# Sharing one pass of the input projection between two prompt tiles and the sample in a decoder layer with an expert stream

## The chip, the cores and the metric
One core of a Trainium2 chip. The metric is the device time of one execution of the kernel, in microseconds, as the median of several runs.

## What is computed
One layer of a decoder for a prompt of 512 tokens and a sample of 8 sequences with 4 new tokens each, width 1024, all in float32:

```python
h = rms_norm(x, norm1) * (1 + sc1) + sh1
zq, zkc, zvc, zks, zvs, zkw, zvw, zg, zglu = split(h @ w_in)     # 1024 -> 2328 columns
# attention: compressed blocks, selected blocks, window; the conv branch: glu, depthwise 31 taps
mix = concat([rms_norm(o_attn), o_conv * scale]) @ w_out
x = x + gt1 * mix
h2 = rms_norm(x, norm2) * (1 + sc2) + sh2
x = x + gt2 * peer(h2)       # per token 8 heads x 16 of 16384 experts: gather u and v rows, dot, gelu, weigh, sum
```

The keys and values, the last 30 columns of the convolution's input, and the layer's rows are outputs. `compress` turns 32 key rows into one through a hidden layer with the weights `cmp_w1` (4 MiB for keys and values).

## The kernel before, in words
The 544 token rows are cut into five tiles: four of the prompt (128 rows each) and the sample (32 rows). Each tile goes through the stages x (norm, modulate, turn), glu, z (q, k, w products, norms, turns), conv, cmp (compression), att (8 heads), mix (output projection and first residual), query0 and query1 (the experts' query projection and scores) and topk0, topk1 (the choice of 128 experts a token). The sample has sc (four parts: compression of the cached pages) and satt in place of cmp and att.

Two streams share the engines. The **expert rows**: GpSimd gathers u and v of one chosen expert for each of 128 tokens (1 MiB, line 1964) into a ring of ten buffers; DVE makes the dot product (line 1920), ScalarE gelu and a diagonal (lines 1400 to 1416), TensorE the weighted sum (line 1053, two rows of the plan at a time), which frees the buffer. One gather is one **row of the plan**: 128 for each prompt tile, 32 for the sample (which packs four heads' groups of 32 tokens), 544 in all. FIRST[i] is the first row of tile i: 0, 128, 256, 384, 512. The **side work**: the stages of the next tile, written as generators that yield at the end of a slot. Each engine runs the same sequence of slots in order, between its instructions for the rows; PE takes its slots four rows ahead.

`make_plan` (L412) lists the stages in windows: a list of lists holds lanes that go side by side. `SLOTS_OF` (L399) gives for each stage its slots and its length in rows, `size_of` that of att by tile (16, 26, 30, 40). `slots_before` (L446) searches a pace so that all lengths together, times the pace, end at row 500; within an item all slots are evenly spaced. An item holding lanes has the length of its first lane. mix of tile i may not begin before row FIRST[i-1] + 8. Tile 0's side work runs before the first row.

Weights come in **units** of 1 MiB (256 columns of a matrix), through three slots; SyncE loads unit j when unit j-3 has been used, in the order of `weight_units`. For every tile these are four glu units, five z units, four compression units, four of `w_out`, eight of `peer_q`, and two half units of keys. `aside` (L2087) hangs everything else that SyncE does on a unit, ahead of its load: `load_x` at a tile's first glu unit, `store_z` and `store_y(i-2)`, `load_y(i-1)` and the modulation rows at its first `w_out` unit. SyncE waits in order, so whatever stands in `aside` holds up the units behind it.

PSUM banks 4 to 7 are the side work's, given in turn to each product (`Products`, L88). `stage_room` is one SBUF area that all stages share by time. At a tile's last row ScalarE and DVE read the sums out of banks 0 to 3 (L1383 to L1910) before PE starts the next tile's rows (the wait on `s_ye`).

## Time and profile before

| what | value |
|---|---|
| median of 3 runs | 2131.38 us |
| lowest and highest | 2120.32, 2132.27 us |
| the profiled execution's own time | 2122.48 us |
| its span on the core | 2120.8 us |
| granted TensorE clock, mean | 0.814 |
| first and last dot product | 263.7 and 2104.4 us from the span's start |
| DMA traffic | 782 MB |

All rows below are of that one profiled execution. A window's line gives for each engine the busy microseconds and the number of instructions that lie in it; TensorE shows two records for every float32 matmul. "DMA share" is the mean busy share of the sixteen DMA engines.

### The profile page before, as it was taken

How to read it: one execution, taken by the hardware profiler on the slowest of the kernel's cores; microseconds unless marked ns; L12 is line 12 of the kernel's file. 1: busy time of each engine (PE TensorE's matmuls, PEld its weight loads, DVE VectorE, ACT ScalarE, POOL GpSimd, SP SyncE). 2: the span in 40 equal slices, each digit the busy share in tenths (PEclk: the TensorE clock that was granted, in tenths of full speed). 3: DMA queues.
4: the chain of work that ended last, by engine and by line, in shares of the span. 5: the costliest groups of instructions: out<-in, count | busy, mean ns of one | idle time of the engine just before them, and what ended most of it. 6: DMA issues, size and time to landing. Idle time of an engine off the chain costs nothing.

```text
span 2120.8 us, 29350 instructions
## 1 busy us (share of the span) xinstructions
PE 1529.5 (72%) x9952; PEld 883.9 (42%) x9952; DVE 1239.4 (58%) x3327; ACT 781.9 (37%) x2225; POOL 698.6 (33%) x611
## 2 busy tenths in 40 slices
PE   6686468777768876868795675989687776769533
PEld 4556335334534444644252353545254332436100
DVE  0151685784686884686797359653555454443754
ACT  2231154662244754255483332252412232332322
POOL 0840122332323432323434232344323333323442
PEclk7877779778978877979797797979888878878765
DMA  7764999988999978999999989999989989999996
GB/s 280 272 251 160 370 375 420 399 315 331 421 415 397 413 326 355 377 386 422 424 386 420 425 365 371 399 419 393 424 319 377 406 327 342 367 413 384 414 413 275
DMA packets 149993, 782.09 MB, mean 369 GB/s; under 512 B 17392, under 2 KB 53136, under 8 KB 60932
## 3 DMA queue, kind: packets, MB, share of 16 engines
q0 software_dynamic: 78336, 570.46, 65.5%
q1 hardware_dynamic: 71509, 209.77, 25.9%
q8 instruction: 80, 1.31, 0.2%
q14 instruction: 68, 0.56, 0.1%
HBM read 773.75 MB, written 10.99 MB: 370 GB/s over the span
## 4 chain that ended last, share of the span: by engine, by line
PE 22%; DMA 13%; DVE 8%; issue 6%; SPq 3%; ACT 3%; POOL 1%; POOLq 0%; ACTq 0%; DVEq 0%
PE bank L1053 9%; DMA expert_rows<-in_expert_uv,expert_index 8%; PE bank L930 5%; DVE expert_rows L1920 3%; PE bank L857 2%; PE bank L841 1%; SPq L2007 1%; PE bank L675 1%; SPq L2002 1%; DMA weight_units<-in_win_values 1%; DMA weight_units<-in_win_keys 1%; DMA weight_units<-in_w_out_units 1%; DMA gate_or_shift_and_scale<-mod_dram 1%; PE bank L647 1%; PE bank L1056 1%
## 5 line engine op out<-in xcount | busy, mean ns | idle before, releaser
L1964 POOL DMA_INDIRECT expert_rows<-in_expert_uv,expert_index x544 | 626.5, 1152 | 1333.9 <-PE bank L1053 1090.0
L1920 DVE CUSTOM_DVE_ANT_0 expert_rows<-expert_rows,h_rows 128x1024 f32<-128x1024 f32 x544 | 658.6, 1223 | 383.2 <-DMA expert_rows<-in_expert_uv,expert_index 376.0
L1053 PE MATMUL bank<-expert_rows,weight_diagonals 64*64 64x512 f32 x4096 | 600.6, 713 | 120.4 <-ACT weight_diagonals L1416 95.2
L1400 ACT ACTIVATE group_gelu<-group_dots 128x2 f32<-128x2 f32 x272 | 55.2, 203 | 788.0 <-DVE group_dots L1920 748.0
L1053 PEld LDWEIGHTS bank<-expert_rows,weight_diagonals 64*64 64x64 f32 x4096 | 152.4, 153 | 396.4 <-issue 223.8
L857 PEld LDWEIGHTS bank<-stage_room,weight_units 128*128 128x128 f32 x1280 | 153.6, 200 | 40.4 <-issue 31.2
L1416 ACT ACTIVATE weight_diagonals<-consts_sb,group_weights 128x64 f32<-128x64 f32 (+1 forms) x544 | 158.1, 338 | 20.0 <-PE bank L1053 2.5
L857 PE MATMUL bank<-stage_room,weight_units 128*128 128x128 f32 (+1 forms) x1280 | 160.7, 286 | 5.7 <-DMA weight_units<-in_peer_q_units 3.1
L1406 ACT ACTIVATE group_weights<-group_gelu,expert_gate 128x1 f32<-128x1 f32 x544 | 130.5, 287 | 9.4
L930 PE MATMUL bank<-weight_units,prompt_bias 128*128 128x256 f32 x512 | 129.5, 404 | 0.0
L1532 DVE SCALAR_TENSOR_TENSOR conv_out<-stage_room,small_weights,conv_out 128x128 f32<-128x128 f32 (+1 forms) x480 | 125.4, 319 | 0.0
L930 PEld LDWEIGHTS bank<-weight_units,prompt_bias 128*128 128x128 f32 x512 | 97.8, 199 | 38.8 <-issue 26.5
L841 PE MATMUL bank<-weight_units,stage_room 128*128 128x256 f32 (+1 forms) x320 | 82.3, 419 | 29.8 <-DVE stage_room L1676 15.4
L1400 ACT ACT_TABLE_LOAD x80 | 102.6, 1283 | 1.4
L675 PE MATMUL bank<-weight_units,stage_room 128*128 128x256 f32 (+1 forms) x400 | 92.5, 386 | 3.1 <-DMA weight_units<-in_w_in_units 3.1
L647 PEld LDWEIGHTS bank<-stage_room,weight_units 128*128 128x128 f32 x640 | 75.3, 197 | 23.4 <-issue 15.9
L841 PEld LDWEIGHTS bank<-weight_units,stage_room 128*128 128x128 f32 (+1 forms) x320 | 60.6, 194 | 56.0 <-DVE stage_room L1676 17.9
L675 PEld LDWEIGHTS bank<-weight_units,stage_room 128*128 128x128 f32 (+1 forms) x400 | 68.6, 176 | 33.7 <-issue 15.2
L647 PE MATMUL bank<-stage_room,weight_units 128*128 128x128 f32 (+1 forms) x640 | 78.5, 283 | 4.3 <-ACT stage_room L1118 3.8
L1056 PE MATMUL bank<-expert_rows,weight_diagonals 128*32 128x512 f32 x128 | 29.1, 1059 | 54.7 <-ACT weight_diagonals L1416 43.3
L1225 ACT ACTIVATE stage_room<-stage_room,stats 128x128 f32<-128x128 f32 (+7 forms) x96 | 44.8, 468 | 50.5 <-DVE stats L1632 50.4
L780 PE MATMUL bank<-prompt_keys_values,queries_turned 64*128 64x128 f32 (+3 forms) x128 | 56.4, 551 | 5.0 <-ACT stage_room L1238 3.4
(253 smaller groups left out, 1606.6 us busy)
## 6 DMA issues: line engine op xcount, KB each, us to landing
weight_units<-in_w_in_units SPq DMA_DIRECT2D x45, 1024.0 KB
weight_units<-in_peer_q_units SPq DMA_DIRECT2D x40, 1024.0 KB
weight_units<-in_w_ada_units SPq DMA_DIRECT2D x24, 1024.0 KB
weight_units<-in_w_out_units SPq DMA_DIRECT2D x20, 1024.0 KB
weight_units<-in_w_units SPq DMA_DIRECT2D x16, 1024.0 KB
expert_rows<-in_expert_uv,expert_index POOLq DMA_INDIRECT x544
weight_units<-in_cmp_pages SPq DMA_DIRECT2D x128, 64.0 KB
gate_or_shift_and_scale<-mod_dram SPq DMA_DIRECT2D x12, 512.0 KB
```

Source lines behind the costliest of these rows:

```text
L647: last = mm(out[:, a * P:a * P + r], w[:, k, a * P:(a + 1) * P], hT(i, k), start=(k == 0), stop=(k == KD - 1))
L675: last = mm(out[0:r, c * 256:(c + 1) * 256], hT(i, k), w[:, k], start=(k == 0), stop=(k == KD - 1))
L841: last = mm(out[0:r, 0:256], e.catT[:, k, 0:r], w[:, k], start=(k == 0), stop=(k == KD - 1))
L857: last = mm(out[:, c:c + r], w[:, k, a * P:(a + 1) * P], e.h2T[:, k, 0:r], start=(k == 0), stop=(k == KD - 1))
L930: last = mm(dst, e.w1_s[:, one, s, hh * P:(hh + 1) * P], w[:, :, :, s], start=False, stop=(one == 1 and s == 7))
L1053: last = mm(e.bank[2 * a + c][o * HD:(o + 1) * HD, :], e.diag[ps, m % (NG * GR)], e.ring[ps, m % RING, cs], start=first, stop=final)
L1400: do(e.act_v[:, p], e.dots[:, p], ACT.Gelu_apprx_tanh).then_inc(e.s_gelu, 1)
L1406: do(e.wv[:, p, j:j + 1], e.act_v[:, p, j:j + 1], ACT.Copy, scale=e.gsm[:, i % 2, o + j:o + j + 1]).then_inc(e.s_w, 1)
L1416: do(e.diag[:, p * GR + j, 0:unit.shape[1]], unit, ACT.Copy, scale=e.wv[:, p, j:j + 1]).then_inc(e.s_d, 1)
L1532: ins = vec.scalar_tensor_tensor(out, src, w[:, ct, k:k + 1], out, ALU.mult, ALU.add)
L1920: vec.tensor_tensor_reduce(out=row, in0=row, in1=e.h2[:, i % 2], scale=1.0, scalar=0.0, op0=ALU.mult, op1=ALU.add, accum_out=e.dots[:, q % ...
L1964: pool.indirect_dma_start(e.ring[:, n % RING], None, e.io["expert_uv"], bass.IndirectOffsetOnAxis(ap=e.eidx[:, i % 2, j:j + 1], axis=0)).t ...
```

## The change
Tiles 2, 3 and the sample ("the team", 288 tokens) are normed one after the other through the one x buffer and go through glu and z together: each glu unit is multiplied with 288 columns at once, each z unit is used for three tiles before it is given back. The compression's four units serve tiles 2 and 3. Tile 3's queries and convolution input wait in DRAM until its attention; the sample's u and queries stay in small tiles; x of the three tiles is loaded again for the residual. All stores of the three tiles' keys and values come ahead of tile 2's first `w_out` unit. The plan's window of tile 3 begins with topk1 of tile 2 and attention 3, beside the convolution; that of the sample begins with sc. Cut to its core:

```diff
+LATE = 2
+TEAM = tuple(range(LATE, TILES))
+TOKENS = sum(rows(t) for t in TEAM)
+
+
+def columns(i, k):
+
+    if i < LATE:
+        return slice(k * P, (k + 1) * P)
+    a = k * TOKENS + (i - LATE) * P
+    return slice(a, a + rows(i))
+
+
+Z_ORDER = ([(n, i) for i in range(LATE) for n in ("q", "k", "w", "cmp")]
+           + [(n, i) for n in ("q", "k", "w") for i in TEAM] + [("cmp", PT - 1), ("sc", 0), ("sc", 1)])
+KEYS_NORMED = [z for z in Z_ORDER if z[0] in ("k", "w")]
+
+
+def keys_normed(name, i):
+    return KEYS_NORMED.index((name, i)) + 1
+
+
+def x_loads(i):
+    return 16 * (i + 1 if i < LATE else TILES + i - LATE + 1)
...
+    team = mods[:].rearrange("p o n -> p (o n)")
+    e.eb_team = team[:, 0:2 * TOKENS].rearrange("p (a n) -> p a n", a=2)
+    e.u3 = team[:, 2 * TOKENS:2 * TOKENS + 4 * P].rearrange("p (c n) -> p c n", c=4)
+    e.q3 = team[:, 2 * TOKENS + 4 * P:2 * TOKENS + 8 * P]
...
+    e.hT = room[:, 0:KD * TOKENS]
+    e.ht = [room[:, 1024:2048]] * LATE + [room[:, 4416:5440]] * len(TEAM)
+    at = [2048] * LATE + [KD * TOKENS + 512 * (i - LATE) for i in TEAM]
+    e.zc = [room[:, a:a + 384] for a in at]
+    e.zw = [room[:, a + 384:a + 512] for a in at]
+    e.sq = [room[:, 2560:3072]] * LATE + [e.convo[:].rearrange("p c n -> p (c n)")] * len(TEAM)
+    e.qr = [room[:, 3072:3584]] * LATE + [e.attn[:]] * len(TEAM)
...
+TEAM_SLOTS = {"glu": (18, 14), "z": (38, 22), "cmp": (15, 8)}
...
-    for i in range(2, PT):
-        windows.append(chain(i, []))
-    windows.append([[[("sc", 0), ("x", PT), ("glu", PT)], [("topk1", PT - 1)]], ("sc", 1), ("z", PT),
+    windows.append(chain(LATE, []))
+    windows[-1][0][0][1:1] = [("x", i) for i in TEAM[1:]]
+    i = PT - 1
+    windows.append([[[("topk1", i - 1), ("att", i)], [("conv", i)]],
+                    ("mix", i), ("query0", i), [[("query1", i)], [("topk0", i)]]])
+    windows.append([[[("sc", 0)], [("topk1", PT - 1)]], ("sc", 1),
                     [[("sc", 2), ("sc", 3), ("satt", PT)], [("conv", PT)]],
                     ("mix", PT), ("query0", PT), ("query1", PT), ("topk0", PT)])
...
+    def glu_team(i):
+        for t in TEAM:
+            prod.freed(pe, ("hT", t, 0))
+            prod.freed(pe, ("hT", t, 1))
+        for ct in range(4):
+            w = units.take(("in", i, 5 + ct)).rearrange("p (k n) -> p k n", k=KD)
+            for a in range(2):
+                out = prod.open(pe, ("glu", i, ct, a))
+                for k in range(KD):
+                    last = mm(out[:, 0:TOKENS], w[:, k, a * P:(a + 1) * P], e.hT[:, k * TOKENS:(k + 1) * TOKENS],
+                              start=(k == 0), stop=(k == KD - 1))
+                    if k == 3:
+                        yield
+                last.then_inc(prod.ready, 1)
+                if a == 0:
+                    yield
+            units.used_by(("glu", i, ct, 1))
+            yield
...
+        new_u(PT - 1)
+        new_u(PT)
+        ws = [unit(0), unit(1)]
+        yield from product("q", ws, LATE, False, False)
+        yield
+        yield from product("q", ws, LATE + 1, False, False)
+        turn_q(LATE)
+        yield
+        yield from product("q", ws, PT, False, True)
+        turn_q(LATE + 1)
+        yield
+        ws = [unit(2), unit(3)]
+        yield from product("k", ws, LATE, False, False)
+        turn_q(PT)
+        yield
+        yield from product("k", ws, LATE + 1, False, False)
+        yield
+        turn_k(LATE)
+        yield from product("k", ws, PT, False, True)
+        yield
+        turn_k(LATE + 1)
+        ws = [unit(4)]
+        yield from product("w", ws, LATE, True, False)
+        yield
+        turn_k(PT)
+        yield from product("w", ws, LATE + 1, True, False)
+        yield
+        turn_w(LATE)
+        yield from product("w", ws, PT, True, True)
+        yield
+        turn_w(LATE + 1)
+        yield
+        yield
+        yield
+        turn_w(PT)
...
+                for t, out in zip(tiles, outs):
+                    lo = blocks_of(t)[0]
+                    for s in range(8):
+                        j = 32 * (s % 4)
+                        last = mm(out[j:j + 32, 0:256],
+                                  e.rT[:, kv, s, lo + one:lo + one + 16].rearrange("p c g -> p (c g)"),
+                                  w[:, s], start=(one == 0 and s < 4), stop=(one == 1 and s >= 4))
+                    if one:
+                        last.then_inc(prod.ready, 1)
+                    elif t == tiles[-1]:
+                        units.used(last)
+                    if not one or t != tiles[-1]:
+                        yield
+            units.used_by(("part", tiles[-1], kv))
+            yield
...
+        if i > LATE:
+            prod.wait(act, ("hT", i - 1, 1))
+        link(do(e.ht[i][0:r], e.x[0:r], ACT.Square, accum_out=e.st[0:r, 0:1]))
...
+        act.wait_ge(e.s_h2, i)
+        for ct in range(4):
+            for _ in range(4):
+                yield
+            out = prod.wait(act, ("glu", i, ct, 1))
+            if ct >= 2:
+                prod.freed(act, ("glu", i, ct - 2, 0))
+            do(e.eb_team[:, ct % 2], out[:, 0:TOKENS], ACT.Sigmoid).then_inc(prod.free(("glu", i, ct, 1)), 1)
...
+        vec.tensor_copy(e.cu[:, :, 0:CK - 1], e.tail[:])
+        for ct in range(4):
+            for _ in range(4):
+                yield
+            prod.freed(dve, ("glu", i, ct, 1))
+            out = prod.wait(dve, ("glu", i, ct, 0))
+            for t in TEAM:
+                dst = e.cu[:, ct, CK - 1:] if t == LATE else e.u3[:, ct] if t < PT else e.us[:, ct]
+                c = slice((t - LATE) * P, (t - LATE) * P + rows(t))
+                ins = vec.tensor_tensor(dst, out[:, c], e.eb_team[:, ct % 2, c], ALU.mult)
+            ins.then_inc(prod.free(("glu", i, ct, 0)), 1)
...
+        elif i < PT:
+            dve.wait_ge(e.s_ul, 16)
+            link(vec.tensor_copy(e.cu[:, :, 0:CK - 1], e.tail[:]))
+        else:
+            dve.wait_ge(e.s_hist, 16)
+            link(vec.tensor_copy(e.cs[:, :, :, CK - 1:], e.us[:].rearrange("p c (b t) -> p c b t", b=NB)))
...
-            if h == 0 and i == PT - 1:
-                dve.wait_ge(e.s_uo, 16)
-            if h == 1 and i == PT - 1:
-                dve.wait_ge(e.s_zo, 16 * e.z_stores[i])
+            if h == 0 and i == LATE:
+                dve.wait_ge(e.s_uo, 16 * (1 + NB))
+            if h == 1 and i == LATE:
+                dve.wait_ge(e.s_zo, 16 * e.z_stores[PT])
...
-    def load_x(i):
-        if i:
+    def load_x(i, again=False):
+        if again and i == LATE:
+            sp.wait_ge(e.s_h, TILES)
+        elif again or 0 < i <= LATE:
             sp.wait_ge(e.s_h2, i)
             sp.wait_ge(e.s_xo, 16 * i)
+        elif i:
+            sp.wait_ge(e.s_h, i)
...
-        if kind == "in" and key[2] == 3 and i >= PT - 1:
-            store_new_u(i)
+        if key == ("in", LATE, 3):
+            store_new_u(PT - 1)
+            store_new_u(PT)
+        if key == ("in", LATE, 6):
+            load_x(LATE + 1)
+        if key == ("in", LATE, 7):
+            load_x(PT)
+        if key == ("pages", 0, 2):
+            sp.wait_ge(e.s_rt, 2 * PT - 1)
+            sp.dma_start(e.cs, io["conv_history"]).then_inc(e.s_hist, 16)
+            prod.wait(sp, ("o", PT - 1, H - 1))
+            sp.dma_start(e.bias_s, io["bias_sample"][:, 0:PAST + WIN]).then_inc(e.s_sb, 16)
...
-            if 0 < i < PT:
+            if i == 1:
                 store_z(i)
+            if i == LATE:
+                for t in TEAM:
+                    store_z(t)
+                sp.dma_start(e.gate_dram, e.gates[PT][0:NS]).then_inc(e.s_gs, 16)
+                prod.freed(sp, ("q", PT - 1))
+                sp.dma_start(e.q_dram, e.q3).then_inc(e.s_spill, 16)
+                sp.dma_start(e.u_dram, e.u3).then_inc(e.s_spill, 16)
+                sp.wait_ge(e.s_gs, 16)
+                for b in range(NB):
+                    src = bass.AP(e.gate_dram.tensor, b * DT * 3 * H, [[3, H], [3 * H, DT], [1, 3]])
+                    sp.dma_start(e.gates_s[b % 4 * 32:(b % 4 + 1) * 32, b // 4, :], src).then_inc(e.s_gs, 16)
+                sp.wait_ge(e.s_spill, 32)
+            if i == PT - 1:
+                prod.wait(sp, (score_parts(LATE)[-1][0], LATE, H - 1))
+                sp.dma_start(e.qT[:], e.q_dram).then_inc(e.s_ql, 16)
+                sp.wait_ge(e.s_tail, 2)
+                sp.wait_ge(e.s_rt, 2 * LATE + 1)
+                sp.dma_start(e.cu[:, :, CK - 1:], e.u_dram).then_inc(e.s_ul, 16)
+            if i >= LATE:
+                load_x(i, True)
```

Left out: the splitting of the z generators of ACT and DVE into functions for one tile and group (the instructions of one tile are the same), the new semaphores, `modT` and `small` areas used for the sample's queries and gates, and the reordering of the `pe` columns.

## Rows read from the trace of the kernel before
**Rows 1.** The page: DMA share in 40 slices, and the two large queues.
```profile
DMA  7764999988999978999999989999989989999996
...
q0 software_dynamic: 78336, 570.46, 65.5%
q1 hardware_dynamic: 71509, 209.77, 25.9%
```

**Rows 2.** Windows: us, busy us (count) by engine, PEclk, DMA share, GB/s.
```profile
264.00:2104.00 1840.00, 1351.04 (x8653) 749.76 (x8653) 1148.79 (x3014) 715.87 (x2047) 616.93 (x534) 0.82 0.95 387
...
510.00:545.00 35.00, 33.21 (x250) 22.77 (x252) 15.47 (x40) 10.62 (x36) 11.51 (x10) 0.88 0.75 300
...
647.00:677.00 30.00, 27.27 (x201) 17.94 (x203) 14.87 (x32) 19.47 (x48) 10.02 (x8) 1.00 1.01 413
...
726.00:760.00 34.00, 25.48 (x117) 14.87 (x117) 24.12 (x68) 19.04 (x50) 5.30 (x7) 0.60 0.62 250
...
929.00:977.00 48.00, 40.69 (x280) 25.86 (x284) 43.33 (x140) 25.07 (x54) 14.20 (x14) 0.87 0.93 378
...
1006.00:1134.00 128.00, 104.81 (x701) 51.64 (x697) 110.34 (x326) 75.05 (x208) 53.72 (x47) 0.88 0.99 406
...
1134.00:1170.00 36.00, 20.53 (x136) 5.73 (x132) 24.45 (x39) 12.17 (x44) 14.93 (x13) 0.68 1.01 427
...
1170.00:1231.00 61.00, 32.87 (x157) 20.36 (x150) 20.22 (x37) 20.00 (x49) 14.53 (x13) 0.76 1.01 423
...
1231.00:1263.00 32.00, 31.28 (x246) 20.66 (x245) 15.21 (x36) 10.40 (x36) 12.37 (x10) 0.93 0.83 330
...
1531.00:1851.00 320.00, 238.12 (x1434) 127.25 (x1438) 157.55 (x382) 81.95 (x277) 103.32 (x90) 0.83 0.93 357
...
1976.00:1998.00 22.00, 9.34 (x52) 2.19 (x48) 21.38 (x60) 6.61 (x18) 8.34 (x8) 0.73 1.00 423
```

**Rows 3.** Waits of the span: us in total, times, longest.
```profile
POOL expert_rows L1964 <- PE bank L1053: 1090.0, 225, 27.5
...
PE bank L1053 <- DVE y_half_sums L1897: 25.1, 3, 9.9
```

**Rows 4.** Groups by line and shape, PE: 597 to 677, then 1310 to 1531.
```profile
L675 PE MATMUL bank<-weight_units,stage_room 128*128 128x256 f32 x80 | 19.5, 398 | 1.1 <-DMA weight_units<-in_w_in_units 1.1
...
L647 PE MATMUL bank<-stage_room,weight_units 128*128 128x128 f32 x128 | 15.4, 278 | 0.9 <-ACT stage_room L1118 0.9
...
L685 PE MATMUL bank<-small_weights,stage_room 128*128 128x24 f32 x16 | 1.9, 264 | 0.0
...
L647 PE MATMUL bank<-stage_room,weight_units 128*128 128x32 f32 x128 | 15.5, 280 | 0.0
...
L675 PE MATMUL bank<-weight_units,stage_room 128*32 128x256 f32 x80 | 18.5, 385 | 0.4 <-DMA weight_units<-in_w_in_units 0.4
```

**Rows 5.** DVE: dots (two instructions each) in windows, and the convolution's group.
```profile
929.00:977.00 48.00, 16.04 (x27) 0.87 0.93 378
...
1006.00:1134.00 128.00, 55.50 (x91) 0.88 0.99 406
...
L1532 DVE SCALAR_TENSOR_TENSOR conv_out<-stage_room,small_weights,conv_out 128x128 f32<-128x128 f32 x120 | 34.9, 344 | 0.0
```

**Rows 6.** PE: the expert rows' products alone, 1006 to 1134.
```profile
1006.00:1134.00 128.00, 51.26 (x356) 13.07 (x360) 0.88 0.99 406
```

**Rows 7.** Issues of SyncE: KB and us to landing; a wait; one store's issue.
```profile
prompt_keys_values<-in_bias_sample SPq DMA_DIRECT2D x1, 768.0 KB, 12.9
...
small_weights<-in_small SPq DMA_DIRECT2D x1, 487.0 KB, 5.2
...
SPq L2082 <- DVE y_rows L1910: 156.5, 1, 156.5
...
1007.42 0.43 SPq L2037 DMA_DIRECT2D out_new_sel_prompt<-stage_room  x1
```

**Rows 8.** DVE's sum of k's squares in tile 2's z, 657 to 663.
```profile
L1544 DVE TENSOR_REDUCE stats<-stage_room 128x2 f32<-128x128 f32 x1 | 0.3, 286 | 6.3 <-ACT stage_room L1159 6.3
```

More of the change, by code:

```diff
@@ L667, in z, with turn_w @@
+    def turn_w(i):
+        r = rows(i)
+        pe.wait_ge(e.s_zn, keys_normed("w", i))
+        out = prod.open(pe, ("w", i))
+        turn(out[:, 0:r], e.zw[i][0:r], ident[0:r, 0:r]).then_inc(prod.ready, 1)
     def z(i):
+        if i == LATE:
+            yield from z_team(i)
+            return
         r = rows(i)
@@ L747, in cmp @@
+            units.used_by(("part", tiles[-1], kv))
+            yield
+        for t in tiles:
+            prod.freed(pe, ("part", t, 1))
+            out = prod.open(pe, ("hid", t))
+            for a in range(4):
+                last = mm(out[:, a * 32:(a + 1) * 32], e.parts[:, t % 2, a // 2, a % 2 * P:(a % 2 + 1) * P],
+                          e.consts[:, C_STACK:C_STACK + NS], start=True, stop=True)
+            last.then_inc(prod.ready, 1)
         yield
-        prod.freed(pe, ("hid", i))
+        i = tiles[-1]
@@ L749, in cmp @@
+        hi = blocks_of(i)[1]
+        for t in tiles:
+            prod.freed(pe, ("hid", t))
         out = prod.open(pe, ("cmp", i))
@@ new lines, in z_team @@
+    def z_team(i):
+        yield
+        for t in (PT - 1, PT):
+            n = CK - 1 if t < PT else NS
+            out = prod.wait(act, ("new_u", t))
+            nc.scalar.copy(e.urow[t], out[0:n, :]).then_inc(prod.free(("new_u", t)), 1)
+        for _ in range(3):
+            yield
+        for t in TEAM:
+            if t > LATE:
+                yield
+                yield
+                q_kept(t - 1)
+                yield
+            q_squares(t)
+            yield
+            root_of(t, "q", slice(40, 48), rows(t))
+        yield
+        yield
+        yield
+        q_kept(PT)
+        for t in TEAM:
+            if t > LATE:
+                yield
+                yield
+                k_turned(t - 1)
+                yield
+            k_kept(t)
+            yield
+            root_of(t, "k", slice(48, 50), rows(t))
+        yield
+        yield
+        for t in TEAM:
+            w_kept(t)
+            yield
+            root_of(t, "w", slice(50, 52), rows(t))
+            yield
+            if t == LATE:
+                k_turned(PT)
+            else:
+                w_turned(t - 1)
+            yield
+        yield
+        w_turned(PT)
@@ L1204, in cmp @@
+        i = tiles[-1]
         yield
```

432 lines of the change are left out of this document (247 added, 185 removed).

## The prediction
> **What bounds the kernel now.** I read the slices and the queues of the page first, to see which resource is full. The DMA slices stand at 9 nearly everywhere behind the start [rows 1], while PE is busy for 73% and DVE for 62% of the part that carries rows [rows 2]. Two thirds of the traffic is the expert rows: 544 gathers of one MiB each take 65.5% of the sixteen engines' time, and everything that SyncE issues takes 25.9% [rows 1]. From the first dot product (264 us) to the last (2104 us) the DMA share is 0.95 [rows 2]: 1748 us of transfers in 1840 us, 92 us of room. So the span there is the transfers plus the time in which none can run, and an edit acts either on the bytes or on that room.
>
> Second the stretches, to see where the room lies. The 28 stretches that I cut at the planner's stage borders (a dot product is one row of the plan, so counting them gives the time of a row) fall into two kinds. Where weights stream beside topk or z the share is 1.01. Room appears where PE is full (query0: 33.21 of 35 us busy, share 0.75; 0.83 for tile 3, 0.83 and 0.86 for the two others), where tile 0's sums are read from the banks at row 128 (34 us at 0.62), and in the sample's attention (320 us at 0.93) [rows 2]. Tile 3's attention runs at 0.99 and the pause behind it at 1.01.
>
> Third the waits. GpSimd waits 1090 us in 225 pieces for PE to free a ring buffer [rows 3]. That does not name PE as the bound: ten buffers hold 25 us of gathers, and while DMA is full they are all in flight or just used.
>
> **What the change removes.** The ring of weight units loses four glu and five z units twice (tile 3, sample) and the four compression units of tile 3: 22 units of 1 MiB, 23.1 MB. Price: the gathers' queue moved 570.46 MB in 65.5% of 2120.8 us, 2.55 us per MiB, SyncE's 209.77 MB in 25.9%, 2.75 us per MiB with its many small packets [rows 1]. I take 2.6: 57 us. It adds the x rows of tiles 2, 3 and the sample a second time (1.125 MiB) and queries and u of tile 3 to DRAM and back (1 MiB): 2.1 MiB, 6 us. **Net 51 us of transfers.** (If nothing limited except DMA this would be the gain.) In a stretch with no weights the engines moved 427 GB/s [rows 2], which makes the net 21 MB worth 49 us, at SyncE's 2.75 us per MiB 55 us; these are the ends.
>
> The Trainium skill ("DMA: Bandwidth & Descriptors", Specifications) puts the HBM limit of a core at about 358 GB/s; by it the 21 MB would be worth 58 us. The 427 GB/s stand above that limit, so the rows decide.
>
> PE gains too. A glu of 128 columns was 128 records (two per matmul) in 15.4 us, 0.12 us each; the sample's with 32 columns took 15.5 us all the same; z's 80 records of 256 columns took 19.5 us, 0.24 each [rows 4]. So the time follows the columns above some 128: one pass with 288 columns is 128 x 0.274 = 35 us in place of 15.4 + 15.4 + 15.5 = 46 us. These 11 us lie beside transfers and count for nothing by themselves; they stand in (b). z keeps all its matmuls, three tiles' worth.
>
> **What it moves.** The planner spreads the side work over rows: before, lengths of 486.5 rows at pace 0.994 plus a pause of 16.6 rows ahead of tile 3's mix (which may not begin before row 264). After, the lengths are 89.5 + 116.5 + 82.5 + 181.5 = 470 at pace 1.064, and no pause. By that plan:
> - rows 95 to 120: x of three tiles and the joint glu, beside topk1 of tile 1;
> - rows 120 to 143: joint z; 143 to 184: both compressions and attention 2;
> - rows 219 to 271: topk1 of tile 2 in the first 31 slots, attention 3 in the last 30, the convolution in the first 43; no weights are needed;
> - everything else is stretched by 7% (rows of its own cost 2.55 us of gather each wherever DMA is full, and come out of the rows that tile 3 and the sample needed).
>
> **Where room for DMA is lost.** (a) Rows 219 to 271, first 26.5 rows. DVE: a dot is 1.22 us (55.50 us for 45.5) [rows 5], 32 us; topk1 is what DVE does in 929 to 977 beyond its dots, 43.33 - 16.04 = 27 us less 2 of glu, 25 us [rows 2, 5]; three quarters of the convolution (34.91 us for 120 of 124 taps) 27 us. Sum 84 us, and DVE has run at most 0.97 full (21.38 of 22 us) [rows 2], so 87 to 89 us; the gathers and some 1.6 MiB of x, q, u, and shift need 72 us. Missing cover: 16 us. The last 25.6 rows, PE: the rows took PE 51.26 us for 45.2 [rows 6], 1.13 each, 29 us; attention 3 is what is left of PE's 104.81 us [rows 2], 53.6, less some 3 of compression; so 80 us against 75 us of transfers: 5 us. Below, the ten-row ring lets DMA run ahead some rows on entering such a stretch, and gives all 21 us back; above, nothing. I take 18, near the upper end: in query0 PE was the bound for 35 us only, and the ring did not bridge even that (share 0.75 [rows 2]).
> (b) Rows 95 to 143. PE: z is 19.5 us a tile and 1.9 for its gates, 19 for the sample [rows 4], turns 5, rows 47.9 x 1.13 = 54, glu 35, x 4, in all 160 us; DMA: 47.9 x 2.55 + 9 units of 2.6 + 3 of x = 149 us. At row 128 PE also waits for the banks, 8.4 us a time (25.1 for 3 [rows 3]); that stall moves from attention 2, where it cost 13 us (34 at 0.62 [rows 2]), into z, where PE is short. So 11 + 8 us here, less what attention 2 no longer loses: I take 10, from 0 to 20.
> (c) SyncE now holds x of tile 3 until tile 2 is normed, the sample's until tile 3 is, and weight units 6 to 8 of glu behind them. Between norm and need lie 3 slots, 3 x 0.79 rows x 3.2 us = 7.6 us. A 768 KB load under this traffic landed in 12.9 us, 487 KB at the start in 5.2 us [rows 7]; 512 KB then 5 to 9. From 0 to 10 us; I take 4.
> (d) The room in the stretches that vanish goes with them: tile 3's glu (48 us at 0.93 [rows 2]) 3 us, and as much taken for the sample's. -6.
> (e) The 29 stores, two spills and their waits go on SyncE ahead of the weights of mix 2, 0.43 us each [rows 7], 15 us in all. They begin behind the first compression unit, and attention 2 asks for them some 40 us later; mix 2's weights have 30 slots. No cost while that cover holds, 10 us if it were halved. Before, SyncE stood 156.5 us at tile 1's y store [rows 7]: that wait stays, with x, q and u now issued ahead of it; nothing behind it is needed before row 267. Its end at row 260 no longer falls on the start of mix 3 (61 us for 10 rows [rows 2]), but DMA was full there (1.01), so it isn't counted twice.
>
> Sum: -51 + 18 + 10 + 4 - 6 = **-25 us**. The profiled execution took 2122.5 us (span 2120.8 and 1.7 around it) and would take 2097.5; it lies 9 us under the median 2131.4, at which the forecast is **2106 us**.
>
> **Rivals.**
> 1. *DMA is the bound throughout*, the ring bridges (a) to (c): -51, **2080 us**. For it: share 1.01 in every stretch with weights and the dense topk; against it: 0.75 to 0.86 where PE was full. 22%.
> 2. *The saved transfers turn into DVE- and PE-bound time*: (a) 21, (b) 20 and (c) 10 at their ends, with (d) nearly eaten by the longer stages: -51 + 51 - 4 = -4, **2127 us**. For it: the pause of 16.6 rows at 2.2 us each was the fastest part of the kernel, and it is gone. 28%.
> 3. *Slower: the joint z exposes its norms.* Nine products (q, k, w of three tiles) each need square, sum, root, scale and turn before their bank is free, through four banks. In tile 2 that took DVE's 6.33 us wait once [rows 8]; the product of two units beside it takes PE 32 x 0.24 = 7.8 us. If ACT's and DVE's slots lag so that none of the nine is covered, 9 x 6.3 = 57 us are added, with row products queued behind PE: -51 + 21 + 57 = +27, **2158 us**. It decides from the point where the chain is longer than one product, and PE would be idle in z, where it was 27.27 of 30 us busy [rows 2]; that speaks against. 8%.
>
> My forecast has 42%.
>
> **How the numbers follow.** The range reaches from near rival 1 to past rival 2 and leaves most of rival 3 out: 2074 to 2140. A change within 1% (21 us) is about what this measurement can't tell from none. Rival 1 and three fifths of my forecast's spread (it sits 4 us past the bound) are faster by over 1%: 0.22 + 0.27 + a little of rival 2 = 0.51. Rival 3 and a tail give slower 0.09; the rest, 0.40, is the same.
>
> **What would show it.** The queue of SyncE moves 209.8 - 21 = 189 MB. In rows 219 to 245 DVE over 0.93 busy with DMA under 0.95; in the joint z PE over 0.9. If DMA stays at 1.0 in both, rival 1 holds. If PE is idle in z for DVE or ACT over 10 us, rival 3. If the DMA share over the rows falls from 0.95 to 0.93 or below with 1700 us of transfers, rival 2. My forecast wants 1697 us of transfers in 1815 us, 0.935. It is wrong if the row-carrying part shrinks by under 10 or over 40 us.

## The result, and the profile after

The changed kernel takes 2112.77 us, the median of 20 runs (2101.95 to 2125.22); the kernel before, run beside it, takes 2136.86 us (20 runs). The ratio on record is 0.9924 (95% interval 0.9905 to 0.9943): 16 us faster (12 to 20), against a forecast of 25. The two medians lie 24 us apart; why that is more than the ratio says is not known. I go by the ratio, which a second timing of the change repeats (experiment 11), so the forecast of 25 is not met by it, though the medians look as if it were. The profiled execution took 2110.55 us with a span of 2108.8, 12.0 less than before; its dot products run from 264.7 to 2092.5 us, 12.9 less.

The changed kernel's page, the slices and queues to be read beside [rows 1]:

```profile
DMA  7764989988999989999888899999899998999996
GB/s 273 281 249 156 363 361 420 416 335 342 380 416 414 350 346 412 421 373 400 359 325 312 353 388 411 350 409 400 329 409 377 358 360 339 350 410 419 382 410 280
...
q0 software_dynamic: 78336, 570.46, 67.1%
q1 hardware_dynamic: 69637, 188.92, 23.8%
```

SyncE's queue lost 20.85 MB, as said (189 MB). But the gathers, with the same bytes, now take 67.1% of 2108.8 us, 1415 us, where they took 65.5% of 2120.8, 1389 us. So the busy share no longer tells how full the queues are, and the GB/s column has to be read beside it. The changed kernel's windows (columns as in [rows 2]), the part with rows first, then the shared x and glu, the joint z, compression with attention 2, query1 with topk0, topk1 with the convolution, attention 3:

```profile
265.00:2092.00 1827.00, 1337.77 (x8384) 727.86 (x8384) 1148.48 (x3016) 700.20 (x2025) 616.45 (x534) 0.82 0.95 378
...
610.00:685.00 75.00, 65.01 (x361) 36.69 (x362) 61.32 (x181) 44.56 (x104) 26.79 (x24) 0.92 1.01 413
685.00:776.00 91.00, 84.54 (x523) 50.81 (x521) 43.69 (x91) 56.14 (x133) 23.04 (x23) 0.98 0.87 338
776.00:895.00 119.00, 96.12 (x721) 47.06 (x717) 100.82 (x314) 70.53 (x204) 56.06 (x43) 0.89 1.01 416
...
979.00:1040.00 61.00, 33.91 (x240) 20.19 (x239) 44.32 (x136) 12.55 (x37) 18.64 (x16) 0.77 1.02 418
1040.00:1123.00 83.00, 46.84 (x214) 11.34 (x214) 82.05 (x256) 19.86 (x71) 28.17 (x24) 0.62 0.84 312
1123.00:1212.00 89.00, 77.67 (x470) 44.01 (x470) 65.04 (x192) 61.84 (x158) 28.82 (x26) 0.82 0.84 326
```

With a share of 1.01 or 1.02 the engines move 413 to 418 GB/s. With 0.84 they move 312 or 326, which is up to 25% less and not 16%. I therefore count **lost time** by bytes: a stretch's length less the time that its bytes take at 415 GB/s, the middle of what the full stretches show. For the part with rows before, 387 GB/s x 1840 us [rows 2] = 712.1 MB or 1716 us, so 124 us lost. After, 378 x 1827 = 690.6 MB or 1664 us, so 163 us lost. (The printed GB/s are whole numbers, so each is good to some 2 us.) The saved bytes are worth 52 us, and 39 us come back as lost time. Three stretches in which DVE or PE is busy for 87% or more lose 57: joint z 338 x 91 = 30.8 MB or 74 us, 17 lost; topk1 with the convolution 21 (DVE busy for 82.05 of 83 us); attention 3 19.

What the forecast had not seen is a wait. The changed kernel's waits of DVE, PE and POOL (1023 to 1060) and of SyncE's queue (979 to 1060), then what SyncE's queue and DVE do there (start, us, what, and in brackets the idle time before it):

```profile
DVE stage_room L1768 <- DMA stage_room<-u_dram: 12.4, 1, 12.4
```
```profile
PE bank L1196 <- ACT weight_diagonals L1654: 24.4, 4, 13.9
```
```profile
POOL expert_rows L2263 <- PE bank L1196: 28.5, 4, 15.4
```
```profile
SPq L2462 <- DVE expert_index L2066: 36.0, 1, 36.0
```
```profile
1023.31 0.62 SPq L2463 DMA_DIRECT2D stage_room<-u_dram  x1
```
```profile
1024.89 0.87 DVE L2021 MAX8 stage_room<-stage_room 128x8 f32<-128x128 f32 x4
1038.20 0.22 DVE L1768 COPY stage_room<-conv_tail 128x120 f32<-128x120 f32 x1 [12.44 <-DMA stage_room<-u_dram]
```

SyncE may load tile 3's u back into `stage_room` only when topk0 of tile 2 has been routed (L2462), so it issues the load at 1023.31. DVE comes to the convolution's first instruction at 1025.8 and stands until 1038.2, with topk1 and the dot products of the expert rows queued behind it. PE then waits for the diagonals that follow from the dots, and GpSimd for PE's buffers. The transfers stop a little later, when the gathers in flight have landed. The changed kernel's DMA view of 1040 to 1123, in 40 slices of 2.1 us, with the gathers' queue; then that queue in 776 to 895:

```profile
GB/s 308 57 0 55 280 379 343 359 415 312 387 324 178 158 411 411 411 430 276 351 324 268 166 383 371 363 375 367 387 426 197 99 367 399 229 367 383 332 422 415
...
q0 software_dynamic: 3446, 25.13, 81.1%
```
```profile
q0 software_dynamic: 5645, 41.09, 82.7%
```

The price of the wait lies in the slices 57, 0, 55 and, as I read it, in the 83 us in which DVE has to work off what it put aside; experiments 2 and 5 test that.

### The profile page after: what moved, and what is told of

The parts are those of the page before. It is cut to its first block, busy times and chain, and to the rows that moved or that the text cites. A ratio compares the mean times of both kernels' runs of the same rounds, so it can differ in the third digit from the quotient of the medians.

```text
span 2108.8 us, 28757 instructions
## 1 busy us (share of the span) xinstructions
PE 1517.9 (72%) x9679; PEld 864.5 (41%) x9679; DVE 1237.0 (59%) x3320; ACT 766.1 (36%) x2202; POOL 698.0 (33%) x611
## 3 DMA queue, kind: packets, MB, share of 16 engines
q0 software_dynamic: 78336, 570.46, 67.1%
## 4 chain that ended last, share of the span: by engine, by line
PE 34%; DMA 29%; DVE 17%; issue 7%; SPq 7%; ACT 5%; POOL 2%; POOLq 0%; ACTq 0%; DVEq 0%
DMA expert_rows<-in_expert_uv,expert_index 16%; PE bank L1196 10%; DVE expert_rows L2219 6%; PE bank L1073 4%; PE bank L1000 3%; PE bank L984 3%; DMA weight_units<-in_win_values 2%; DMA gate_or_shift_and_scale<-mod_dram 2%; DVE conv_out L1782 2%; PE bank L737 2%; SPq L2306 2%; DMA weight_units<-in_w_ada_units 2%; SPq L2301 2%; POOL expert_rows L2263 2%; SPq L2294 1%
## 5 line engine op out<-in xcount | busy, mean ns | idle before, releaser
L1000 PEld LDWEIGHTS bank<-stage_room,weight_units 128*128 128x128 f32 x1280 | 153.8, 200 | 35.3 <-issue 32.8
L1000 PE MATMUL bank<-stage_room,weight_units 128*128 128x128 f32 (+1 forms) x1280 | 160.4, 285 | 1.0 <-ACT stage_room L1527 1.0
L984 PE MATMUL bank<-weight_units,stage_room 128*128 128x256 f32 (+1 forms) x320 | 79.8, 410 | 11.1 <-DVE stage_room L1975 9.4
L984 PEld LDWEIGHTS bank<-weight_units,stage_room 128*128 128x128 f32 (+1 forms) x320 | 59.0, 188 | 38.8 <-DVE stage_room L1975 13.4
L737 PE MATMUL bank<-weight_units,stage_room 128*128 128x256 f32 (+1 forms) x240 | 55.1, 383 | 2.3 <-issue 2.3
L1034 PE MATMUL bank<-consts_sb,h_rows 128*128 128x128 f32 (+1 forms) x40 | 8.9, 400 | 56.9 <-DVE h_rows L1999 56.9
L1069 PE MATMUL bank<-weight_units,prompt_bias 128*128 128x2 f32 x32 | 6.1, 261 | 60.3 <-issue 54.4
L943 PEld LDWEIGHTS bank<-prompt_keys_values,stage_room 128*128 128x128 f32 x320 | 42.6, 210 | 15.0 <-issue 14.6
```

The source lines that it names most:

```text
L737: last = mm(out[0:r, c * 256:(c + 1) * 256], hT(t, k), w[:, k], start=(k == 0), stop=(k == KD - 1))
L984: last = mm(out[0:r, 0:256], e.catT[:, k, 0:r], w[:, k], start=(k == 0), stop=(k == KD - 1))
L1000: last = mm(out[:, c:c + r], w[:, k, a * P:(a + 1) * P], e.h2T[:, k, 0:r], start=(k == 0), stop=(k == KD - 1))
```

## The experiments

Each ratio is to the kernel before, timed on the same chip; 0.001 of it is 2.1 us. Stretches of different kernels are compared over the same rows of the plan, found by counting dot products. A *slot* is one step of a stage's generator; a stage's *length* is given in rows of the plan.

**1. The bytes alone.** The kernel before without the 22 loads that the change removes; nothing else is moved. The products that would use them work on the units that stand in the slots, so tile 3's and the sample's values are others.

```diff
+def reloaded(key):
+    return not (key[0] == "in" and key[1] >= 3 or key[0] == "w1" and key[1] == 3)
...
+            if not reloaded(key):
+                return
```

> The kernel before, with the 22 unit loads left out that the change saves (tile 3's and the sample's input projection, tile 3's compression): PE multiplies with whatever lies in the slot, everything else, the plan too, is as before. So this is the saved traffic alone, without the change's schedule and without its added transfers. If the bytes are worth their transfer time wherever they stood (my theory: they stood in stretches with a DMA share of 0.96 to 1.01, and the change lost part of it again in new stretches), it is 45 to 57 us faster than before, ratio 0.973 to 0.979. If the bytes themselves were hidden in good part (rival: the traffic was never worth more than what the change gained), it is 15 to 30 us faster, ratio 0.986 to 0.993, and the change's schedule cost nothing.

Measured: 2103.70 us, ratio 0.9885 (0.9851 to 0.9919), 25 us, less than half of the 56 us that 23.1 MB are worth at 415 GB/s. This is in the range of the second reading, though not for its reason: the bytes were not hidden before, other engines took their place, as the stretches show. Its windows, the part with rows, then tile 3's glu with topk1, its z, its compression and attention; and tile 3's z before:

```profile
265.00:2082.00 1817.00, 1342.10 (x8653) 751.16 (x8653) 1145.85 (x3014) 715.61 (x2047) 629.22 (x534) 0.83 0.94 379
924.00:971.00 47.00, 39.81 (x280) 25.67 (x284) 43.54 (x142) 25.07 (x54) 16.22 (x14) 0.89 0.71 265
971.00:998.00 27.00, 25.04 (x174) 16.28 (x166) 14.75 (x30) 17.55 (x45) 7.48 (x7) 1.00 0.83 326
998.00:1123.00 125.00, 100.99 (x709) 49.98 (x705) 108.84 (x326) 75.45 (x210) 51.11 (x47) 0.90 0.99 393
```
```profile
977.00:1006.00 29.00, 26.27 (x190) 16.71 (x186) 14.28 (x30) 18.14 (x47) 8.20 (x8) 1.00 1.01 426
```

Glu was 48 us at 378 GB/s [rows 2] and is 47 at 265: the transfers are gone and the stretch stays, with DVE busy for 43.54 of it. z was 29 us and is 27 (PE 25.04). Over the rows 379 x 1817 = 688.6 MB or 1659 us, so 158 us are lost instead of 124. A share of 1.01 had said that DMA was full; it had not said that without the transfers glu would shorten by only 1 us and z by only 2. (The values that differ also change which experts are gathered. Experiment 6, with other values too and every load, stays at 0.9981, so that by itself brings little.)

**2. The convolution later.** The changed kernel with tile 3's convolution begun 18 slots later.

```diff
-    windows.append([[[("topk1", i - 1), ("att", i)], [("conv", i)]],
+    windows.append([[[("topk1", i - 1), ("att", i)], [("gap", 18), ("conv", i)]],
```

> The changed kernel, with the convolution of tile 3 begun 18 slots later in its window (it ends with attention 3, in slot 61), nothing else. In the changed kernel DVE is 82 of 83 us busy while it does topk1 and three quarters of the convolution, and DMA moves 312 GB/s there; then PE is the fuller engine. If DVE's order is what costs in the first half, the first half falls from 83 us to some 72 to 75, the second stays near 89 (DVE there 65 plus 15 us of taps), so 5 to 10 us faster than the changed kernel: ratio to before 0.988 to 0.990. If the stretch of 52 rows is bound as a whole (rival), it gives back in the second half what it gains in the first: ratio 0.992, as the change.

Measured: 2094.92 us, ratio 0.9831 (0.9804 to 0.9857), 20 us better than the change by the ratios, and with experiment 9 the fastest version here that leaves nothing out. Both expectations missed it: they looked at the two halves of attention 3's window (74 and 91 us, where 72 to 75 and 89 were expected), and not at the stretch ahead of them, where DVE had stood waiting. Its windows: the rows, joint z, query1 with topk0, topk1, attention 3.

```profile
265.00:2077.00 1812.00, 1338.71 (x8384) 731.70 (x8384) 1147.47 (x3017) 699.83 (x2025) 615.32 (x534) 0.82 0.96 381
683.00:778.00 95.00, 86.87 (x522) 52.61 (x520) 43.30 (x91) 56.11 (x133) 23.08 (x22) 0.95 0.82 323
984.00:1031.00 47.00, 31.92 (x232) 20.10 (x235) 42.63 (x132) 12.55 (x37) 16.85 (x14) 0.86 1.01 419
1031.00:1105.00 74.00, 44.41 (x226) 10.80 (x218) 69.84 (x206) 19.88 (x71) 31.54 (x26) 0.68 1.02 419
1105.00:1196.00 91.00, 73.51 (x474) 40.50 (x470) 79.23 (x245) 62.43 (x159) 29.66 (x27) 0.88 0.83 323
```

The same rows of the plan take 47 us and 74 us instead of 61 and 83, and topk1 now runs at the full rate; attention 3 takes 91 us instead of 89. Lost over the rows: 1812 us less 1664 (381 x 1812 = 690.4 MB), 148 us. That is 14 us less than in the changed kernel: topk1's stretch loses 21 us less, joint z 4 us more (323 x 95 = 30.7 MB or 74 us, 21 lost), attention 3 one more. Joint z has the same instructions in both; its granted clock was 0.95 instead of 0.98, and PE was busy for 86.87 us instead of 84.54.

**3. Attention 3 longer.** The changed kernel, with attention 3 given a length of 52 rows of the plan instead of 40, so that more gathers lie beside it.

```diff
-        return 30, (16, 26, 30, 40)[i]
+        return 30, (16, 26, 30, 52)[i]
```

> The changed kernel, with the planned length of attention 3 raised from 40 to 52 rows; the pace falls from 1.064 to 1.037 and all other stages come 2.5% closer together. The window of topk1, attention 3 and convolution then has 63 rows instead of 52 for the same DVE and PE work, so DVE's and PE's share of a row falls and DMA should be full again there. My theory (room is lost because side work without any weights is packed into too few rows): 5 to 15 us faster than the change, ratio 0.985 to 0.990. Rival (the loss only moves, since the other stages are now packed more tightly): within 3 us of the change, 0.991 to 0.994.

Measured: 2129.33 us, ratio 0.9967 (0.9936 to 0.9999), some 9 us slower than the change, with intervals that just overlap, where one reading expected a gain and the other none. Its window over the rows:

```profile
265.00:2114.00 1849.00, 1348.82 (x8380) 733.44 (x8380) 1144.33 (x3006) 696.31 (x2023) 609.67 (x534) 0.82 0.94 374
```

374 x 1849 = 691.5 MB or 1666 us, 183 us lost (the traced execution, 2135.11 us, lies 6 us above the median). In the 52 rows that are topk1 and attention 3 in the changed kernel 26 us are lost instead of 40; all others, packed closer, lose 158 instead of 123. DVE's wait for u was in it too, 11.4 us.

**4. Joint z longer.** The changed kernel, with joint z given a length of 28 rows instead of 22.

```diff
-TEAM_SLOTS = {"glu": (18, 14), "z": (38, 22), "cmp": (15, 8)}
+TEAM_SLOTS = {"glu": (18, 14), "z": (38, 28), "cmp": (15, 8)}
```

> The changed kernel, with the planned length of the joint z raised from 22 to 28 rows (pace 1.050). PE is 84.5 of 91 us busy in it and DMA stands at 338 GB/s. If the joint z is bound by PE, six rows more let DMA be full: some 6 to 10 us less room there, ratio 0.988 to 0.991. If what it loses is the pause at row 128 (PE waits for the banks to be read, which comes whatever the length), it stays at 0.991 to 0.993.

Measured: 2119.68 us, ratio 0.9946 (0.9922 to 0.9969), some 5 us slower than the change by the ratios, which the overlapping intervals don't tell from none, where one reading expected a gain. The wait for u was in it too, 12.6 us.

**5. The convolution a little later.** As 2, with 5 slots: enough to cover the load of u, while DVE's work stays nearly where it was.

```diff
-    windows.append([[[("topk1", i - 1), ("att", i)], [("conv", i)]],
+    windows.append([[[("topk1", i - 1), ("att", i)], [("gap", 5), ("conv", i)]],
```

> The changed kernel, with the convolution of tile 3 begun 5 slots later (13 us), not 18. In the changed kernel DVE stands 12.4 us at the first instruction of that convolution, for tile 3's u to come back from DRAM, with topk1 and the dots queued behind it; beginning 18 slots later brought 18 us. Theory A (the wait for u is the larger part): the 5 slots already hide the wait, so 9 to 13 us faster than the change, ratio 0.986 to 0.988; the rest up to 0.983 is DVE's crowd in the first half. Theory B (DVE's crowd of topk1 and taps is the larger part): 0 to 5 us faster than the change, ratio 0.990 to 0.992.

Measured: 2099.91 us, ratio 0.9844 (0.9821 to 0.9866), 17 us better than the change, with intervals well apart, and more than either reading expected (9 to 13 us if the wait was the larger part). The other 13 slots of experiment 2 add nothing beyond the intervals. Its wait for u, and its windows (rows, joint z, query1 with topk0, topk1 with the convolution, attention 3):

```profile
DVE stage_room L1768 <- DMA stage_room<-u_dram: 1.1, 1, 1.1
```
```profile
265.00:2087.00 1822.00, 1330.99 (x8384) 725.56 (x8384) 1147.27 (x3017) 700.28 (x2025) 621.47 (x534) 0.82 0.95 379
683.00:779.00 96.00, 87.66 (x525) 53.08 (x523) 44.22 (x91) 56.11 (x133) 23.12 (x23) 0.95 0.83 324
984.00:1030.00 46.00, 30.31 (x220) 18.56 (x223) 42.57 (x132) 12.55 (x37) 15.70 (x13) 0.80 1.01 419
1030.00:1112.00 82.00, 45.78 (x226) 10.58 (x218) 79.98 (x245) 20.10 (x72) 32.17 (x26) 0.65 0.98 385
1112.00:1205.00 93.00, 78.24 (x470) 42.84 (x470) 68.93 (x205) 62.68 (x158) 27.91 (x26) 0.83 0.80 307
```

DVE is as full as in the changed kernel (79.98 of 82 us), and only some 2 us of its work have moved out, so most of the gain is the wait's; no run removes the wait and leaves all else in place. DVE's work of 84 us was foreseen, and the stretch loses 6 us here (385 x 82 = 31.6 MB or 76 us), not 21. (This profiled run, 2105.00 us, lies 5 us above its median. So its trace shows 1822 us over the rows against the change's 1827, less of a gain than the ratios.)

**6 and 7. Less PE work.** The kernel before, and that of experiment 1, with half of the products of tile 3's and the sample's glu and z left out (k below 4 alone).

```diff
+def kd(i):
+    return KD // 2 if i >= 3 else KD
...
-                for k in range(KD):
+                for k in range(kd(i)):
```

> The kernel before with every unit loaded, but only half of the products (k under 4) of tile 3's and the sample's glu and z computed: some 35 us of PE less, in stretches where the DMA share is 0.93 to 1.01. If DMA alone bounds those stretches: within 4 us of before, ratio 0.998 to 1.000. If PE binds there as much as DMA (the 22 units alone brought only 25 of 57 us, and tile 3's z then stood at PE 0.92): also little, since DMA stays; 0 to 8 us, 0.996 to 1.000. It is needed beside the next run.

> The kernel before with the 22 unit loads left out and half of the products of tile 3's and the sample's glu and z left out as well. If the 22 MiB were worth only 25 us because PE (0.92 busy in tile 3's z) and DVE (0.93 in its glu) stood right behind DMA, taking some 35 us of PE as well brings 8 to 18 us more than the loads alone did: ratio 0.980 to 0.984, more than the sum of the two separate runs. If the bytes are cheap for another reason (gathers slow down when they are alone, or the time is set elsewhere), the products add what they added with the loads in place: ratio 0.986 to 0.989.

Measured: all loads, 2128.96 us, 0.9981 (0.9953 to 1.0008). Without the 22 loads, 2104.04 us, 0.9851 (0.9825 to 0.9876); this overlaps experiment 1's interval, so the totals decide nothing: the first ratio is where both of its readings put it, the second lies between its two. The stretches decide. Tile 3's glu and z, first with all loads, then without them:

```profile
930.00:976.00 46.00, 32.25 (x204) 17.25 (x204) 42.54 (x138) 24.49 (x53) 14.53 (x14) 0.79 0.93 383
977.00:1006.00 29.00, 22.94 (x178) 11.83 (x174) 14.80 (x30) 18.13 (x47) 9.41 (x10) 0.91 1.01 426
```
```profile
922.00:968.00 46.00, 31.28 (x203) 16.55 (x201) 42.54 (x134) 25.06 (x54) 15.37 (x14) 0.79 0.65 262
968.00:990.00 22.00, 19.87 (x142) 10.76 (x142) 14.91 (x32) 17.22 (x45) 7.16 (x7) 0.92 1.00 400
```

With all loads z stays at 29 us although PE has 3 us less to do: DMA sets it. Without the loads it goes from 27 to 22 us as PE goes from 25.04 to 19.87: PE had set it. Glu goes from 47 to 46 us with 8.5 us less of PE, and DVE stays at 42.5: that leaves DVE. From tile 3's end to the end of the sample's attention, counted by dot products, both kernels got longer in stretches where little or nothing had been taken away (compression of the pages and the attention of the sample, some 14 and 21 us together). In the sample's attention the granted clock was 0.79 instead of 0.83 in the first, but 0.81 in the second as in experiment 1, so it isn't the clock alone. I have no cause for it; it is left open.

**8. Joint z with less PE work.** The kernel of experiment 2 with half of the sample's products in the joint z left out.

```diff
-                for k in range(KD):
-                    last = mm(out[0:r, c * 256:(c + 1) * 256], hT(t, k), w[:, k], start=(k == 0), stop=(k == KD - 1))
+                kd = KD // 2 if t == PT else KD
+                for k in range(kd):
+                    last = mm(out[0:r, c * 256:(c + 1) * 256], hT(t, k), w[:, k], start=(k == 0), stop=(k == kd - 1))
```

> The changed kernel with tile 3's convolution 18 slots later (0.983), and in the joint z only half of the sample's products (40 records of 0.24 us, 9.7 us of PE less). PE is 84.9 of 93 us busy there and DMA stands at 320 GB/s. If the joint z is bound by PE: 6 to 10 us faster than that kernel, ratio 0.978 to 0.980. If what is lost there is the banks' reading at row 128 and the chains of the norms: 0 to 3 us, 0.982 to 0.983.

Measured: 2085.42 us, ratio 0.9772 (0.9743 to 0.9801), 12.6 us less than experiment 2, with intervals that barely don't touch. The joint z:

```profile
682.00:772.00 90.00, 77.64 (x481) 48.01 (x479) 42.75 (x90) 56.15 (x133) 22.53 (x22) 0.95 0.89 343
```

95 us became 90 as PE went from 86.87 to 77.64. So PE's work sets a part of joint z: some half of the 9.2 us taken off it shows in the stretch, at the same granted clock of 0.95. The total fell by more than the 6 to 10 us expected of a joint z bound by PE, and by more than the traces show: 1806 us over the rows against 1812. The rest of the 12.6 us is not placed.

**9 to 11. The rest of the plan.** The kernel of experiment 2 with attention 3 given a length of 34 rows, the same with joint z given 28 instead (attention again 40), and the changed kernel once more, all on one chip.

```diff
-        return 30, (16, 26, 30, 40)[i]
+        return 30, (16, 26, 30, 34)[i]
```
```diff
-TEAM_SLOTS = {"glu": (18, 14), "z": (38, 22), "cmp": (15, 8)}
+TEAM_SLOTS = {"glu": (18, 14), "z": (38, 28), "cmp": (15, 8)}
```

> The changed kernel with the late conv (ratio 0.983 to before), and the pack of tile 3's attention given a length of 34 instead of 40, so that the transfers of later stages are moved less beside the stretch in which PE and DVE, not the DMA queues, set the pace. Theory A (a stage whose engine time exceeds its positions keeps its time, and what it does not move has to be moved by the stages behind it, which run at the full share): the attention stretch has 323 GB/s, PE 74 and DVE 79 of 91 us in it; with 6 positions less its time stays near 86 to 91 us, and the stages behind move about 14 us more: ratio 0.985 to 0.995, slower than the late conv by 4 to 20 us. Theory B (the attention given 52 lost 9 us without the late conv, so its mirror gains some): 0.977 to 0.981.

> The changed kernel with the late conv, and the joint multiplication of tile 3's and the sample's z given 28 positions instead of 22. The same change without the late conv lost 4 us (0.9946 against 0.9924). Theory A (the joint z is bound by PE, 84.9 of 93 us, as taking half of the sample's products away showed with 12.6 us less; more positions beside it let 6 more rows of reads pass in the same time, and the loss of the first try came from where the wait for u and topk1 then fell): 0.977 to 0.981, that is 4 to 13 us faster than the late conv. Theory B (the z stretch itself gets longer by as much as its added rows take, as it was 102 us for 29 rows against 91 for 23): 0.983 to 0.988, no gain.

> The changed kernel once more, on the chip of the two others, so that their distances can be read side by side. It was at 0.9924 of before (0.9905 to 0.9943). Expected 0.990 to 0.995, with the wait of DVE for u of some 12 us at the first instruction of tile 3's conv in it again.

Measured: 2092.51 us, 0.9831 (0.9802 to 0.9861); 2099.41 us, 0.9868 (0.9833 to 0.9902); and 2109.06 us, 0.9924 (0.9894 to 0.9954), the change's ratio again, as expected. The wait for u in the last one, and its joint z, topk1 with the convolution, and attention 3:

```profile
DVE stage_room L1768 <- DMA stage_room<-u_dram: 12.0, 1, 12.0
```
```profile
678.00:770.00 92.00, 85.58 (x535) 51.31 (x537) 44.65 (x94) 56.31 (x134) 22.80 (x24) 0.98 0.85 339
1038.00:1120.00 82.00, 47.20 (x214) 10.73 (x206) 81.01 (x250) 19.78 (x67) 28.93 (x25) 0.60 0.85 308
1120.00:1213.00 93.00, 83.42 (x470) 46.27 (x470) 64.99 (x184) 61.38 (x158) 27.64 (x26) 0.78 0.81 317
```

Two traces of the same kernel thus agree on the first two (17 and 21 us lost in both) and differ by 4 us on attention 3, where PE was busy for 83.42 us at a clock of 0.78 instead of 77.67 at 0.82, with DVE's work the same. So the length of attention 3 follows PE at least in part, and differences of a few microseconds between single traces are not to be read.

Both expectations for attention missed: 34 rows are worth what 40 are. z with 28 brings nothing, late convolution or not, as its second reading expected, which ends the reading that the wait for u had spoiled experiment 4. The stretch of the rows that are joint z in the change, with 28, and then with 34 for attention the part with rows and the rows that are attention 3 in the change:

```profile
680.00:771.00 91.00, 85.06 (x516) 50.86 (x509) 42.07 (x84) 50.05 (x123) 25.83 (x24) 0.98 0.89 349
```
```profile
265.00:2072.00 1807.00, 1326.48 (x8384) 719.79 (x8384) 1147.48 (x3016) 695.81 (x2023) 621.40 (x534) 0.83 0.96 383
1098.00:1196.00 98.00, 76.42 (x461) 42.96 (x461) 80.05 (x251) 69.47 (x174) 28.47 (x25) 0.83 0.82 320
```

With 28, those rows take 91 us instead of 95, and other stretches take the 4 us back. With 34, the attention's rows take 98 us instead of 91 (the output projection begins in them), others are shorter, and over all rows it is 1807 us against 1812: no difference that can be measured.

## Why the prediction was right, and where it was wrong

The measured time lies in the range and faster than before, as forecast. The gain is 16 us by the ratio and 13 in the row-carrying part of the trace, where 25 were forecast; the prediction called itself wrong under 10. Its terms miss by more than its sum, since they err both ways. By lost time (at 415 GB/s) they compare so, always from one traced execution; the last two columns are experiments 5 and 2, the change without its wait.

| term | forecast | the change | conv 5 slots later | conv 18 slots later |
|---|---|---|---|---|
| bytes | -51 | -52 | -52 | -52 |
| (a), (d) topk1, attention 3, and the stretches that vanish | +18 - 6 | +33 | +23 | +12 |
| (b) joint z, less attention 2 | +10 | +3 | +8 | +8 |
| (c) x in series | +4 | 0 | 0 | 0 |
| elsewhere (the remainder) | 0 | +3 | +3 | +4 |
| over all rows | -25 | -13 | -18 | -28 |

(a) and (d): 20.6 + 19.1 us are lost there after; before, tile 3's glu lost 4.3 and its attention 2.8 [rows 2]. In experiment 5 it is 5.9 + 24.2 in place of the 39.7, in experiment 2 -0.7 + 20.2. (b): joint z loses 16.9 us, and tile 3's z of before, at 426 GB/s, lost none. The 34 us at 250 GB/s at row 128 [rows 2] lost 13.5, and after, the stretch of attention 2 runs at 416 and loses nothing.

**Bytes.** Right as a sum, but not what they bring alone: experiment 1 had -57 us of bytes and +34 of lost time. Rival 1, DMA as the bound throughout, falls with that and with experiments 7 and 8 (6 alone would fit it). The forecast was right to expect that DVE and PE take part of the gain, and (a) and (b) were placed where they are: DVE at 82.05 of 83 us, PE at 84.54 of 91 in joint z, which answers to "PE over 0.9".

**The step that failed** is (e): "No cost while that cover holds", and, of SyncE's order, "that wait stays, with x, q and u now issued ahead of it; nothing behind it is needed before row 267". It asked what is late behind u in SyncE's queue, and not when u itself may be issued and who stands for it. The wait was 12.4 us on the engine with the least to spare, and cost up to 17 us by the ratio of experiment 5. Over all rows the forecast's -25 stands between the -18 and the -28 of the two traces without it. In (a) with (d), missed by 21 us, 10 of the 21 go with 5 slots of room; the other 11 go only with 18, which moves DVE's work as well. How much of them is the wait's can't be told from single traces. Its size was within reach of the prediction only in part: (c) allowed 5 to 9 us for 512 KB under this traffic, and the 256 KB of u took 14.8 us. (a)'s own working held as a sum only: of the 18, from 16 + 5, experiment 5 shows 6 in topk1's stretch and 24 in attention 3's, experiment 2 none and 20. The 75 us of transfers beside attention 3 are not worked out in it (25.6 rows at 2.55 us are 65), and the stretch moved 326 x 89 = 29.0 MB or 70 us. Attention 3 takes 89 to 93 us where 80 were forecast from PE's work; PE is busy for 74 to 83 of them (experiments 2 and 11), so that "PE bound" describes it only in part. What else holds it is open: making it longer or shorter in the plan (experiments 3 and 9) brought nothing, and no run took work off it.

**(b)** was right in kind, with its offset in attention 2 at the 13 us that it named and joint z at 17 or 21 us where 19 were forecast. By its own terms the sum is 11 + 8 - 13 = 6 and not the 10 that it took, and 6 is nearer to the +3 and +8. PE's glu of 288 columns, forecast at 35 us, took 32.9. The changed kernel's PE groups of 610 to 776:

```profile
L737 PE MATMUL bank<-weight_units,stage_room 128*128 128x256 f32 x160 | 36.7, 383 | 2.3 <-issue 2.3
L691 PE MATMUL bank<-stage_room,weight_units 128*128 128x288 f32 x128 | 32.9, 411 | 0.0
```

**(c)** did not show: the stretch of the three norms runs at 413 GB/s.

**Rivals.** The DMA share over the rows is 0.95, which would have refuted both the forecast (0.935) and rival 2 (0.93). By bytes the rate is 378 GB/s, between the 381 that 1815 us would give and the 376 of rival 2's 1836. The share was the wrong gauge. Rival 2 in its own form (every saved transfer turned into bound time, -4) didn't come, but the outcome lies about half way to it. Rival 3, exposed norms in joint z, didn't come: PE was busy for 84.54 of 91 us. (In the chances, three fifths of 0.42 are 0.25, not 0.27; the step to 0.51 then takes 0.04 of rival 2.)

## What to carry to other kernels

When a queue is full, look at how far behind it the next engine stands in each stretch that the saved bytes leave: bytes are worth their transfer time only as far as that, which was less than half of it in experiment 1. When a tensor is spilled and read back, find three times: when its place is free, when its load can be issued after that, and when the first instruction that reads it stands at the head of its engine; put the reader behind the load's landing, not the place's release. A few slots of room in the plan ahead of such a reader may be all it takes: here 5 slots brought 17 us, and moved hardly any engine time.

## What was not expected of the hardware

A gather's packets can take longer in a stretch where the stream stops and starts. In 776 to 895 the changed kernel's gathers moved 41.09 MB in 82.7% of 119 us, 2.40 us per MB; in 1040 to 1123 25.13 MB in 81.1% of 83 us, 2.68 us per MB. So a share of 0.84 went with three quarters of the full rate. That stopping is the cause is not shown: in the kernel before, around the pause at row 128 (726 to 760), they took 2.46, little more than the 2.41 of experiment 2's topk1, which has no pause (94.7% of 74 us for 29.08 MB); and over the whole span all 570.46 MB took 1389 us before, 1415 after and still 1411 in experiment 2.

The load of u, 256 KB, landed 14.8 us after its issue, with the queues full; in experiment 2 another took 14.5. The Trainium skill ("DMA: Bandwidth & Descriptors", Anatomy of one DMA) fits a transfer of the software queue as 2.0 us and its bytes at 436 GB/s. That fit is for the other kind of queue, GpSimd's; carried over to this load of SyncE as an estimate, 256 KB would take 2.6 us. The trace is far from that while gathers are in flight, and that is the difference between a wait that one would not see and the one that was there.
